# Second block's attention run amid its last query pieces and its first output pieces (one core)

## The reference, cut to what matters

```python
def chunk_band_attention(u, k_pad, v_pad, w_q, w_o, rel_bias):
    """Each chunk of queries attends to its own chunk and the 8 previous chunks."""
    q = (u @ w_q).reshape(bsz, n_chunks, CHUNK, B_HEADS, B_HEAD_DIM)
    ...
        s = jnp.einsum('bqhd,bkhd->bhqk', qc, kb).astype(jnp.float32) * scale + bias
        s = jnp.where(valid, s, MASK_VALUE)
        p = jax.nn.softmax(s, axis=-1).astype(vb.dtype)
        return jnp.einsum('bhqk,bkhd->bqhd', p, vb)
    ...
    return o @ w_o
# in the second layer
u = modulate(rms_norm(h, norm_mix[layer]), sh1, sc1)
h = h + g1[:, None, :] * chunk_band_attention(u, k_pad, v_pad, b_w_q[j], b_w_o[j], b_rel_bias[j])
u = modulate(rms_norm(h, norm_ffn[layer]), sh2, sc2)
```

## Time and profile before

| what | value |
|---|---|
| three timed runs | 1589.01, 1589.38, 1591.5 us (median 1589.38) |
| the profiled execution, its own time | 1587.78 us |
| its span in the profile | 1585.7 us |
| PE busy / DVE / ACT / POOL | 95% / 47% / 37% / 2% of the span |
| chain that ended last | 79% PE, 10% DMA, 7% DVE, 3% ACT |

### The profile page before, as it was taken

One profiled execution on the slowest core, in us unless ns is written; L12 is line 12 of the kernel. 1 busy time (PEld: TensorE's weight loads), 2 busy tenths in 40 slices (PEclk: granted clock), 3 DMA queues, 4 the chain that ended last, 5 costly groups with the idle time before them and its releaser, 6 DMA issues.

```text
span 1585.7 us, 26563 instructions
## 1 busy us (share of the span) xinstructions
PE 1505.1 (95%) x11356; PEld 1247.4 (79%) x11356; DVE 743.4 (47%) x1185; ACT 581.7 (37%) x899; POOL 28.0 (2%) x47
## 2 busy tenths in 40 slices
PE   7999998999998979999999899989899999999996
PEld 4988898999998649999999768979666656566553
DVE  4658667677767335545555635644221212222121
ACT  3522243444444445444446625542121222212121
POOL 0100000000000001000000000001000000000000
PEclk9999999999989799999999779999999999999998
DMA  9778447978868404555534313716599999999995
GB/s 365 248 237 286 143 135 282 328 269 298 298 222 298 130 1 142 197 186 184 181 114 133 129 37 101 292 54 240 229 418 424 422 420 424 422 420 425 420 420 222
DMA packets 168467, 404.15 MB, mean 255 GB/s; under 512 B 5013, under 2 KB 131250, under 8 KB 155058
## 3 DMA queue, kind: packets, MB, share of 16 engines
q1 hardware_dynamic: 166336, 397.43, 67.4%
q0 software_dynamic: 1648, 5.18, 1.1%
q10 hardware_dynamic: 386, 0.11, 0.0%
HBM read 401.63 MB, written 1.07 MB: 254 GB/s over the span
## 4 chain that ended last, share of the span: by engine, by line
PE 79%; DMA 10%; DVE 7%; ACT 3%; issue 1%; SPq 1%; DVEq 0%; ACTq 0%
PE ps L1797 27%; PE ps L2332 11%; PE ps L2045 7%; PE ps L2354 5%; DMA arena<-in_w 4%; PE ps L1832 4%; PE ps L1810 3%; PE ps L2319 3%; DMA late<-in_w 2%; PE ps L2077 2%; PE ps L1977 2%; PE ps L1906 2%; PE ps L1896 2%; PE ps L2365 1%; DMA arena<-in_mod_w 1%
## 5 line engine op out<-in xcount | busy, mean ns | idle before, releaser
L1797 PE MATMUL ps<-u,wsplit 128*128 128x256 f32 x3912 | 485.9, 285 | 8.5 <-DVE wsplit L1147 6.9
L1797 PEld LDWEIGHTS ps<-u,wsplit 128*128 128x128 f32 x3912 | 477.0, 193 | 16.5 <-DVE wsplit L1147 8.7
L1147 DVE TENSOR_TENSOR wsplit<-arena,wsplit 128x1024 fp32r<-128x1024 f32 x258 | 312.1, 1222 | 255.6 <-ACT wsplit L759 253.9
L759 ACT ACTIVATE wsplit<-arena 128x1024 fp32r<-128x1024 f32 x258 | 270.7, 1056 | 334.2 <-PE ps L1797 161.5
L2332 PE MATMUL ps<-arena 128*64 128x256 f32 x1408 | 156.9, 380 | 4.8 <-DMA arena<-in_w 4.0
L2332 PEld LDWEIGHTS ps<-arena 128*64 128x64 f32 x1408 | 101.2, 137 | 65.9 <-issue 13.6
L2045 PE MATMUL ps<-hid,wsplit 128*128 128x256 f32 x1056 | 130.2, 283 | 0.3 <-DVE hid L1387 0.3
L2045 PEld LDWEIGHTS ps<-hid,wsplit 128*128 128x128 f32 x1056 | 128.2, 192 | 0.5 <-DVE hid L1387 0.5
L1703 DVE TENSOR_TENSOR arena<-arena,ps 128x256 f32<-128x256 f32 x32 | 13.5, 422 | 244.0 <-ACT arena L1106 244.0
L1111 ACT ACTIVATE arena<-ps 64x512 f32<-64x512 f32 x64 | 37.9, 592 | 145.3 <-PE ps L2354 144.5
L1832 PE MATMUL ps<-wsplit,u 128*128 128x256 f32 x672 | 84.9, 288 | 0.0
(11 more groups left out here) (352 smaller groups left out, 1441.1 us busy)
## 6 DMA issues: line engine op xcount, KB each, us to landing
arena<-in_w SPq DMA_DIRECT2D x66, 2048.0 KB, 25.1
late<-in_w SPq DMA_DIRECT2D x30, 2048.0 KB, 25.6
arena<-in_mod_w SPq DMA_DIRECT2D x48, 1024.0 KB, 6.5
arena<-in_ffn_w_in SPq DMA_DIRECT2D x44, 1024.0 KB, 5.3
arena<-in_ffn_w_out SPq DMA_DIRECT2D x22, 1024.0 KB, 5.0
arena<-in_a_w_in SPq DMA_DIRECT2D x16, 1024.0 KB, 8.6
arena<-in_kv_mod_w SPq DMA_DIRECT2D x8, 1024.0 KB, 4.9
arena<-in_kv_w SPq DMA_DIRECT2D x8, 1024.0 KB, 8.2
```

The lines of the kernel that those rows point to most:

```text
L759: act.activation(piece_buf(p, 0), piece_src(p), ACT.Copy).then_inc(hi_done, 1)
L1147: dve.tensor_tensor(piece_buf(p, 1), piece_src(p), piece_buf(p, 0).bitcast(F32), ALU.subtract).then_inc(lo_done, 1)
L1797: mm = pe.matmul(o, w_[:, k, :], u[:, x_, k, :], start=first, stop=last)
```

## The change

The 16 heads are spread over other products of TensorE. The first four pieces of `b_q` come first, with the row sums and the columns among them; the other four stand behind the scores of the first heads and behind the steps of heads 0, 1 and 2. From step 5 on, every step is followed by six products of the first two pairs of `b_o`, which take the chunk of the attention's output that is ready by then; those pairs are so added up over 16 small portions, and their last two chunks come after the last head. The last two pairs of `b_o` follow as whole pieces. ACT drains the output chunks straight into `u`, DVE makes the remainders in the loop, and the eight copies and eight remainders after the loop go; so does the separate `bo_hi`/`bo_lo` pair of semaphores. The row slots move one place forward in the list of loads, so that only one of them is left for the time after "mix1".

```diff
-ROWS_AT = (2, 3, 4, 5, 6, 7, 8, 9)
+ROWS_AT = (1, 2, 3, 4, 5, 6, 7, 8)
...
-            pool.wait_ge(bo_lo, 8)
+            pool.wait_ge(at_lo, 8)
...
-            for n, pair in enumerate(pairs("b_q")):
+            def queries(pair):
+                n = pairs("b_q").index(pair)
                 result(pair)
                 act.activation(qB[:, 2 * n:2 * n + 2, :], bank(pair), ACT.Copy, scale=0.125).then_inc(lin_out["act"], 1)
+            queries(pairs("b_q")[0])
+            act.wait_ge(rows_mm, 3)
+            act.activation(late_rows, ps[:, 4:6, :], ACT.Copy).then_inc(rows_sb, 1)
+            queries(pairs("b_q")[1])
+            def amid_b(i):
+                if i == 0:
+                    hi_upto(jobs["b_q"][7]["w"])
+                elif i in (1, 3):
+                    queries(pairs("b_q")[(i + 3) // 2])
+                elif i == 4:
+                    hi_upto(jobs["b_o"][3]["w"])
+            def out_hi(i, o):
+                if i == 1:
+                    act.wait_ge(piece_done, LAST["b_q"] + 1)
+                return act.activation(u[:, 0, i // 2, :], o[:, 0:T], ACT.Copy)
...
-            act.wait_ge(piece_done, LAST["b_q"] + 1)
-            attention_act("B", lambda i, o: act.activation(qB[:, i // 2, :], o[:, 0:T], ACT.Copy))
-            act.wait_ge(at_hi, HB // 2)
-            for c_ in range(DC):
-                act.activation(u[:, 0, c_, :], qB[:, c_, :], ACT.Copy).then_inc(bo_hi, 1)
+            attention_act("B", out_hi, amid_b)
...
-            splits("b_q")
-            lo_upto(LAST["b_q"] + LOOKAHEAD)
-            attention_dve("B", None)
+            lo_upto(jobs["b_q"][1]["w"])
+            weighted_rows(jobs["rows_kv"][-1])
+            lo_upto(jobs["b_q"][6]["w"])
             last_gains()
-            for c_ in range(DC):
-                dve.wait_ge(bo_hi, c_ + 1)
-                dve.tensor_tensor(u[:, 1, c_, :], qB[:, c_, :], u[:, 0, c_, :].bitcast(F32), ALU.subtract)\
-                    .then_inc(bo_lo, 1)
+            def amid_b(i):
+                if i == 0:
+                    lo_upto(jobs["b_q"][7]["w"])
+                elif i in (2, 4, 5):
+                    lo_upto(jobs["b_o"][(0, 2, 3)[(2, 4, 5).index(i)]]["w"])
+            attention_dve("B", lambda i, o: dve.tensor_tensor(
+                u[:, 1, i // 2, :], o[:, 0:T], u[:, 0, i // 2, :].bitcast(F32), ALU.subtract), amid_b)
...
-            linears(jobs["b_q"], (u_lo, 24))
+            linear_pair(jobs["b_q"][0:2], (u_lo, 24))
             pe.wait_ge(x_tc, 2)
             row_sums(2, ps[:, 4, :])
             row_sums(3, ps[:, 5, :]).then_inc(rows_mm, 1)
+            linear(jobs["b_q"][2])
+            columns(late_rows[:, 0, :], 4, modps[:, 80:96])
+            columns(late_rows[:, 1, :], 4, modps[:, 96:112]).then_inc(gemv_col, 1)
+            linear(jobs["b_q"][3])
...
+            def out_chunk(c_, n):
+                pair = pairs("b_o")[n]
+                if c_ == 0:
+                    pe.wait_ge(lo_done, pair[1]["w"] + 1)
+                    pe.wait_ge(lin_out[pair[0]["engine_before"]], pair[0]["turn_before"])
+                pe.wait_ge(at_lo, c_ + 1)
+                for p in pair:
+                    for m, (lo, x_) in enumerate(((0, 0), (0, 1), (1, 0))):
+                        mm = pe.matmul(lin[p["out"] % 2][:, p["half"], :], piece_buf(p, lo)[:, c_, :], u[:, x_, c_, :],
+                                       start=(c_ == 0 and m == 0 and p["half"] == 0),
+                                       stop=(c_ == DC - 1 and m == 2), skip_group_check=True)
+                    if c_ == DC - 1:
+                        mm.then_inc(piece_done, 1)
+            def amid_b(i):
+                if i < 3:
+                    linear(jobs["b_q"][5 + i])
+                elif i >= 5:
+                    out_chunk((i - 5) // 2, (i - 5) % 2)
...
-            project("b_o", "ffn1", (bo_lo, 0), follows=jobs["gate1_0"])
+            for n in range(2):
+                for c_ in (6, 7):
+                    out_chunk(c_, n)
+            for n in (2, 3):
+                for p in pairs("b_o")[n]:
+                    linear(p)
+                sums("ffn1", [0, 1] if n == 2 else [2])
+            warm(jobs["gate1_0"], 3)
+            sums("ffn1", [3])
+            warm(jobs["gate1_0"], 1)
```

More of the change, by code:

```diff
@@ L487, in lo_before @@
         def lo_before(k):
-            return k - 12
+            return k - 4
         FILL = jobs["ck"] + jobs["cv"]
@@ L519, in two_blocks @@
         x_n = sem("x_n")
-        bo_hi, bo_lo = sem("bo_hi"), sem("bo_lo")
         flip = part(12288, P)
@@ L729, in _ @@
                                pattern=[[0, 8], [-1, P]], channel_multiplier=1).then_inc(w_ms, 1)
-            pool.wait_ge(at_lo, 4)
+            pool.wait_ge(at_lo, 12)
             pool.memset(turned, 0.0).then_inc(m_const, 1)
@@ L980, in memory @@
                     drained[0] += 1
-            act.wait_ge(rows_mm, 3)
-            act.activation(late_rows, ps[:, 4:6, :], ACT.Copy).then_inc(rows_sb, 1)
-            act.wait_ge(piece_done, LAST["b_q"] + 1)
-            attention_act("B", lambda i, o: act.activation(qB[:, i // 2, :], o[:, 0:T], ACT.Copy))
-            act.wait_ge(at_hi, HB // 2)
-            for c_ in range(DC):
-                act.activation(u[:, 0, c_, :], qB[:, c_, :], ACT.Copy).then_inc(bo_hi, 1)
+            attention_act("B", out_hi, amid_b)
             hi_upto(jobs["b_o"][0]["w"] + LOOKAHEAD)
@@ L1419, in last_gains @@
                 dve.wait_ge(gemv_col, 5)
-                dve.tensor_tensor(mod[:, 80:112], ps[:, 0, 0:32], vec1[:, 80:112], ALU.add).then_inc(mod_done, 1)
+                dve.tensor_tensor(mod[:, 80:112], modps[:, 80:112], vec1[:, 80:112], ALU.add).then_inc(mod_done, 1)
                 dve.wait_ge(mod_done, 11)
@@ L2060, in _, with attention_pe @@
             ffn_pe(0, "ffn0")
-            def attention_pe(kind, keys, queries, values, chunks, bias=None, between=lambda i: None):
+            def attention_pe(kind, keys, queries, values, chunks, bias=None, between=lambda i: None,
+                             arriving=lambda i: None):
                 first, n = FIRST[kind], COUNT[kind]
@@ L2070, in scores @@
                         pe.wait_ge(at_e, 2 * (a - 1))
+                    arriving(i)
                     o = ps[:, 2 + i % 2, :]
@@ L2097, in outputs @@
                         pe.wait_ge(at_hi, k - 1)
-                        if kind == "X":
-                            pe.wait_ge(at_lo, lo_before(k - 1))
+                        if kind != "W":
+                            pe.wait_ge(at_lo, k - 1 if kind == "B" else lo_before(k - 1))
                     pt = pt_sb[:, i % 2, :]
@@ L2158, in memory, with queries_there @@
                         linear_tokens(FILL[n:n + 2])
-            wait_out(pe, jobs["b_q"][-1])
+            def out_chunk(c_, n):
[16 more added lines that the diff above has]
+                    out_chunk((i - 5) // 2, (i - 5) % 2)
+            def queries_there(i):
+                if i % 4 == 0:
+                    wait_out(pe, jobs["b_q"][i // 2])
             pe.wait_ge(b_rel, 96)
@@ L2163, in _ @@
             half = lambda t_, i: t_[64 * (i % 2):64 * (i % 2) + 64, i // 2, :]
[L2164 to L2168, removed]
             attention_pe("B", lambda i, k: half(kB, i), lambda i, k: half(qB, i),
-                         lambda i, b, m: vB[:, b, 64 * i:64 * i + 64], 1, lambda i: biasB[:, i, :], late_columns)
-            pe.wait_ge(mod_done, 12)
-            project("b_o", "ffn1", (bo_lo, 0), follows=jobs["gate1_0"])
+                         lambda i, b, m: vB[:, b, 64 * i:64 * i + 64], 1, lambda i: biasB[:, i, :], amid_b,
+                         queries_there)
+            for n in range(2):
[8 more added lines that the diff above has]
+            warm(jobs["gate1_0"], 1)
             ffn_pe(1, "ffn1")
@@ L2278, in _ @@
                          lambda i, b, m: vX[:, b, T * i + P * m:T * i + P * (m + 1)], 2)
-            pe.wait_ge(at_lo, 4)
+            pe.wait_ge(at_lo, 12)
             project("co", "moe", None, follows=jobs["co"][4:])
```

## The result

| | before | after |
|---|---|---|
| median of 20 timed runs each | 1586.09 us (1572.60 to 1595.28) | 1575.63 us (1569.60 to 1580.02) |
| ratio | | 0.9944, 95% interval 0.9924 to 0.9964 |
| profiled execution: own time, span | 1587.78, 1585.7 us | 1571.75, 1569.8 us |

The change makes the kernel faster: by 10.5 us between the medians, by 8.9 (5.7 to 12.1) by the ratio. I had forecast 6.8 less than 1589.4, 1582.6 us, with 1577.5 as the lowest that I expected. The time lies under the range, and the gain came out larger; by the ratio's interval, though, a gain of 6.8 is not excluded.

A forecast was written before the change was run, and what follows sets the result against it. PE was taken as the bound, losing time to waits and a spell of low clock. Full-clock gain -11.2, load slot +1.0 and clock +3.4 gave -6.8: 1589.4 to 1582.6 us, range 1577.5 to 1588.8.

The forecast's parts named there:

- The schedule at full clock: PE's work from b_q to the first sum after b_o, laid out anew: ending at 607.6 instead of 618.8.
- 2.0 and 1.35: PE's forecast waits in us before the turnings of heads 4 and 5, in steps 3 and 4.
- 0.7 and 2.5: PE's forecast waits in us before pieces 4 and 5 of b_o, counted from 0, after the attention.
- So 11.2 are won at full clock: From b_q to the first sum after b_o, PE was to finish 11.2 us earlier with no low clock.
- I take 3.4 in all: Low clock behind the waits at heads 4 and 5 (2.5) and near the end (about 0.9): 3.4 us lost.
- the clock holds: Rival: no fall of the clock behind the new waits; gain 10.2, time 1579.2 us; chance 0.27.
- I take 1.0: One more load slot ahead of the second b_q slot delays it by 1.0 us, between 0 and 3.0.
- The sum: Whole change: -11.2 + 1.0 + 3.4 = -6.8 us.
- The base: The time of the kernel before, 1589.4 us, to which the forecast change of -6.8 was added.
- the slot 3.0 late: Rival: the second b_q slot lands 3.0 late, not 1.0, same clock; gain 4.8, time 1584.6 us; chance 0.13.
- the gain eaten by ACT's queue: Rival: further waits on ACT in steps 3 to 6 and after the last head leave 1589 us; chance 0.08.
- low clock through the portions: Rival: 0.50 clock from step 5 on costs 3.6 per step; six such steps give 1600.8 us; chance 0.09.

The follow-up runs named there:

- the third execution: The kernel before, unchanged, profiled a third time: 111.51 us from the first b_q product to the first sum of squares after b_o, against 117.35 in its first profile.
- the added copy: Changed kernel plus one unused ACT copy ahead of the last b_q pair; first b_q product to first sum after b_o took 111.76 us, against 105.80.
- the second execution of before: The kernel before, unchanged, profiled again: 123.04 us from the first b_q product to the first sum of squares after b_o, against 117.35 in its first profile.
- the one with 2.89: Changed kernel with the row slots' loads in their old places and a second row slot weighed behind the first b_q pair; ratio 0.9963 to the kernel before.

## Why the prediction was too cautious, step by step

- **The schedule at full clock**: right, its parts less exactly than their sum. The stretch was to be 106.2 (607.6 - 501.4) and is 105.80: the last output ended at 85.6 of it for 86.9, and the end took 20.2 for 19.3, as the first sums behind the sixth piece are 16 products (1.84), not the 8 (0.95) that I had counted. Other parts: waits of 1.88 and 0.95 for 2.0 and 1.35; steps of 3.54 for 3.56; 1.63 and 1.19 in the second half of `b_o` for 0.7 and 2.5, so the sum is right (2.82 for 3.2) and the split is not. I had put one copy in front of the fifth piece and two waits in front of the sixth, where the fifth waited longer for DVE's addition, the releaser of the row.
- **"So 11.2 are won at full clock"**: right against the profile that I had, wrong as a statement on the kernels. Only 5.7 is won at full clock. The rest was a fall of the clock in that execution of before. I had read that fall as 5.0, from steady steps; against the same steps of the third execution it is 5.84. The falls average 5.8 over three, so the number held by luck; against the third execution it would have been twice too large.
- **"I take 3.4 in all" for the clock**: the step that failed. The changed kernel's four profiles lose 0, 2.35, 0.95 and 0 in the stretch, 0.8 in the mean, and nothing at the tail, where 1.00 held behind waits of 1.63 and 1.19. A fall when it came cost what I had said (2.35 for 2.5). But I priced as certain what comes in part of the executions, and put 0.9 for a fall at the end, where none came. That is 2.6 too little gain. The rival "the clock holds" named a gain of 10.2; the medians differ by 10.5.
- **"I take 1.0" for the slot**: 0 (54.1 against 54.0). The gap in front of the full windows took up about half of it (289 GB/s for 216); how the rest was hidden stays open. The Trainium skill, page "DMA: Bandwidth & Descriptors", "Issuing engines are not separate DMA queues", by which I had said that the whole 3.0 would be paid, tells that all loads share the 16 engines. The runs don't contradict that; what they contradict is my step from sharing to no room.
- **The sum**: these two terms are 2.6 + 1.0 = 3.6 of the 3.7 between -6.8 and -10.5. The agreement to 0.1 is better than means of three and four profiles deserve.
- **The base**: the other 3.3. I added the change to 1589.4, the median of three runs; that of twenty is 1586.1, and they spread over 23 us. The range's lower end, 1577.5, took that base as exact, and so did not hold a gain that was forecast to within 4.
- **The rivals**: the slot 3.0 late, the gain eaten by ACT's queue, and low clock through the portions did not come. For the last one, steps 6 to 13 have no wait in any profile with portions, and from step 7 on the clock is 1.00 in all of them (only behind the added copy is it still low in step 6). The Trainium skill, page "TensorE: Matmul & The Clock Gate", "A second HAM failure mode: psum-queue depth-cycling", speaks of another kernel, whose clock goes up and down where PE idles often and shortly. The portions take such idle times away. The steps of before, which have 0.65 in each, hold 1.00 too in all three profiles from 566 on at the latest. The rule did not show in the steady steps of either kernel.

## What to carry to other kernels

Lay the change out at full clock on both sides, and take a low spell in the profile before out of the gain: it is a term with a chance of its own, not work that the change removes. Where the same code takes 10 us more or less from one execution to the next, ask for more than one profile, and widen the range by the base. When work is pulled between the steps of a loop, look at what stands in front of the loop's own step on each helper engine: moving the copies one step ahead took another 1.6 off the stretch here, and the sixth piece's copy 1.5.

## What the runs showed of the hardware

The clock's fall is not a fixed answer to a wait. Behind the same two waits (1.37, 1.44) it came in three of four profiles and cost 5.84, 11.53 and none in the three of one kernel; behind 1.88 it came in four of seven; behind waits of at most 0.65 alone, in none of two. It came in the one profile with 2.83 and the one with 2.89, and in none of ten behind the 1.62 or 1.63 in the second half of `b_o`, so the length of a wait alone does not order them. In the second execution of before it stayed at 0.50 from 540 to 560 though PE was busy without a break (4.00 of 4.00 in the window at 540 above): at half clock PE is the later engine there, and the waits of 0.65 disappear. What decides between the executions these runs do not tell.
